# A two-layer hybrid trunk on one core: the modulation stream, the first norm and the front in one block, and the tail of y in the next pair's levels

## The chip, the cores and the metric

The kernel runs on one core of a Trainium2 chip. The metric is the device time of one execution in microseconds (us). Engines: TensorE (PE), VectorE (DVE), ScalarE (ACT), GpSimd (POOL), and SyncE (SP), which issues the DMAs. Each engine takes its instructions in program order; they wait for one another through semaphores.

## The reference

Two layers over a context of 128 tokens and a sample of 512 tokens (T = 640 columns here), width 1024. All in float32.

```python
m = silu(cvec) @ w_mod + b_mod                     # 6 parts of 1024 for each layer
sh1, sc1, gt1, sh2, sc2, gt2 = split(m, 6)
h = rmsnorm(x, norm_mix) * (1 + sc1) + sh1         # the sample also has grid_posemb added to x
# layer 0
proj = h @ w_in;  r, k, v, u = split(proj)         # u: 256 channels, the Fourier mixer's
dh = centred_shift(h) - h
xw, xa, xg = (h + dh * mu_wag[s] for s in range(3))   # go into three low-rank products
ys, s_fin = wkv7_scan(...)                         # 12 heads of 64, forward and backward
y = ys[0] + flip(ys[1])
y = (y - mean(y)) * rsqrt(var(y) + GN_EPS) * gn_w + gn_b      # over each head's 64 channels
bonus = sum(r * k * r_k) * v
out_a = (y + bonus) * (sigmoid(xg @ g1) @ g2)
out_b = real(fft2(u))                              # over tokens and the 64 channels of a group
x = x + gt1 * (concat(out_a, out_b) @ w_out)
# then a mixture of 16 experts; layer 1 has another mixer; a last norm
```

## The kernel before

Channels lie on the 128 partitions: `x` and `h` are [128, 8 chunks, 640]. The program is a row of blocks, and a block starts when every engine has ended the one before.

**setup().** SyncE loads `vec` (160 KB), `cst` (136), the tables (817) and the masks `m32` (768 KB), then 24 slabs of `mod_w` of 2048 KB, each half of one part's 1024 rows, into a ring of six; `x` (2560 KB) after the twelfth. TensorE takes each slab in 8 products with the two conditioning columns (L266) into PSUM rows; ScalarE copies a finished part (L242), TensorE turns it into columns in 8 products (L253, `turn`), VectorE adds the bias (L298). GpSimd adds the position table to `x` (L324, L326). After the last turn, ScalarE squares `x` chunk by chunk (L124) and TensorE sums the squares over the channels in 40 products of one column (L132).

**norm(0, 0).** VectorE and ScalarE make a rate for each token, TensorE spreads the rates over the partitions (L346), VectorE scales `x` into `h`, ScalarE applies gain and shift.

**even_front().** SyncE loads `w1` (1536 KB), `wu` (1024), `dfs` (2048), `dfp` (128) and saves `x`. TensorE computes the 256 channels of `u` (L462, the channel products), transforms them along the width (L470), multiplies the three mixes by `w1` (L482, the low-rank products) and transforms along the tokens (L490, L492). VectorE makes `dh` and the three mixes for all 8 chunks at a time (L435 to L448). ScalarE copies.

**even_heads().** Six pairs of heads, the first five in a loop with `following`, the last apart. For each pair: matrices of all five tiles of 128 tokens (L707), which VectorE masks (L1150, 20 masks); six **levels** of a block-wise inversion, 30 steps of products of 64 (L744, L748), each put in place by a predicated copy of VectorE (L1156), with one chunk of the next pair's key projection (`project(K, 0, ...)`, L639) after every third step; corners (L782); then a **chain** over four steps of tiles: old state (L806, L809) into `rs`, products for `us` (L817), new state (L827, L828), with pieces of the next pair's work (`FILL`, `ahead`) between them; then `y` into PSUM banks 6 and 7 (`pair(3)`). `pair(q)` is banks 2q and 2q + 1. The tail of y before:

```python
dve: yc = y - mean (L1206); [queries() of the next pair]; reciprocal(root) (L1212)
     yc*root (L1214); yc*gn_w+gn_b (L1216); yc+bon (L1218); mix = yc*pair(0) (L1221)
     sem_inc("tail_done"); bonus() of the next pair (L1128, L1129)
pe:  gate -> pair(0); mean -> pair(2); bonus -> pair(1); variance -> pair(3) (L848 to L853)
```

In the next pair TensorE waits for `tail_done` before its third product of `heads`, since its matrices go to banks 4 to 7, and for `bonus_read` before it writes to `pair(1)`.

Of the kernel before, what the change touches and what calls it, by code (L numbers as in the profile page):

```python
# [69 lines left out]
def build(nc, t):  # L70
    ctx = ExitStack()
    with ctx:
# [44 lines left out]
        chunk_sums = ps[:, 7, 384:384 + KC * NT]  # L117
# [10 lines left out]
        def sum_x(pe, sq, m):  # L128

            pe.wait_ge(sem("xsq_ready"), 1).then_inc(sem("xsq_ready"), -1)  # L130
            for tt in range(NT):
                last = pe.matmul(chunk_sums[:, m * NT + tt:m * NT + tt + 1], sq[:, m % 2, tt * P:(tt + 1) * P], mean1024[:, 0:1], start=True, stop=True)  # L132
            last.then_inc(sem("xsq_used"), 1)
# [69 lines left out]
        def setup():  # L203
            cv = Carve()
            ring = cv(6, 4, 1024)
            th = cv(KC, 2)
            scond = cv(KC, 2)
            rows = cv(3, D)
            m32 = cv(LEVELS * 4 * HD)
            sq = cv(2, T)  # L210
            modw = t["mod_w"]

            with stage() as block:
                @block.sync
                def _(sp):
                    sp.dma_start(vec[:, :], t["vec"]).then_inc(sem("vec_in"), 16)
                    sp.dma_start(cst[:, :], t["cst"][:, 0:NKEEP]).then_inc(sem("const_in"), 16)
                    sp.dma_start(work["tables"][:, :], t["cst"][:, NKEEP:]).then_inc(sem("const_in"), 16)
                    sp.dma_start(m32, t["m8"]).then_inc(sem("const_in"), 16)
                    sp.sem_inc(sem("slab_free"), 6)  # L220
                    for l in range(2):
                        for i in range(2):
                            for s in range(3):
                                for k in range(2):
                                    sp.wait_ge(sem("slab_free"), 1).then_inc(sem("slab_free"), -1)
                                    src = modw[l, k * 512:(k + 1) * 512, :].rearrange("(c p) (i s n) -> i s p c n", p=P, i=2, s=3)
                                    sp.dma_start(ring[:, 2 * s + k], src[i, s]).then_inc(sem(f"slab{2 * s + k}"), 16)
                        if l == 0:
# [4 lines left out]
                def _(act):  # L233
# [9 lines left out]
                    for m in range(KC):  # L243
                        square_x(act, sq, m)
# [1941 lines left out]
```

## Time and profile before

| what | us |
|---|---|
| three runs | 2872.93, 2877.30, 2892.89; median 2877.3 |
| the profiled execution, its own time | 2877.23 |
| its span | 2874.5 |
| setup with its column sums, to the first norm | 0 to 164 |
| norm and front | 164 to 259 |
| six pairs of heads | 259 to 1184 |
| output projection, experts, second layer, last norm | 1184 to 2874 |
| from pair to pair: loads of the gate's weights at 454.00 and, four pairs on, 1034.45 | 145.1 each |
| TensorE, VectorE, ScalarE, GpSimd busy | 2437.3, 1796.3, 1250.9, 158.4 |

### The profile page before, as it was taken

The page shows a single profiled execution, that of the slowest core. Times are in us where ns is not written, and L with a number is a line of the kernel's source. Part 1 is how long each engine was busy: PE and PEld are TensorE (multiplying, and loading weights), DVE is VectorE, ACT ScalarE, POOL GpSimd, SP SyncE. Part 2 cuts the span into 40 slices and gives each one's busy share as a digit, 9 for nine tenths or more (in the row PEclk, how much of TensorE's full clock was granted, in tenths as well). Part 3 has the DMA queues.
Part 4 walks back from the last instruction along what each step waited for, and adds up shares of the span by engine and source line. Part 5 has one row for each costly group of instructions (what it writes and reads, how often), then busy time and mean ns, then how long its engine had stood idle before and what let it go on. Part 6 is the DMA issues. An engine that isn't in the chain of part 4 may idle for free. (4 is left out here: it accounts for less than half of the span.)

```text
span 2874.5 us, 51159 instructions
## 1 busy us (share of the span) xinstructions
PE 2437.3 (85%) x19268; PEld 1642.4 (57%) x19268; DVE 1796.3 (62%) x2258; ACT 1250.9 (44%) x1535; POOL 158.4 (6%) x159
## 2 busy tenths in 40 slices
PE   5668787878787876785999999959988599999995
PEld 1244465656565656453666666645545366666664
DVE  0041646464646462127999999937832799999992
ACT  0120232313131311025888888820122587888881
POOL 0100000000000000001000000000000100000000
PEclk8869898889898887787999999959998799999996
DMA  9921101010101000236999999931102699999992
GB/s 392 372 104 26 26 3 28 3 27 3 27 3 27 3 2 3 96 114 253 374 389 386 388 388 386 345 128 39 59 1 111 248 377 387 386 386 388 386 354 82
DMA packets 172542, 539.20 MB, mean 188 GB/s; under 512 B 12449, under 2 KB 43809, under 8 KB 172258
## 3 DMA queue, kind: packets, MB, share of 16 engines
q1 hardware_dynamic: 165858, 514.62, 46.9%
q0 software_dynamic: 6528, 22.29, 3.3%
q8 instruction: 123, 2.02, 0.3%
q14 instruction: 33, 0.27, 0.0%
HBM read 510.28 MB, written 26.61 MB: 187 GB/s over the span
## 5 line engine op out<-in xcount | busy, mean ns | idle before, releaser
L1652 DVE TENSOR_TENSOR wl<-raw,wh 128x1024 fp32r<-128x1024 f32 x768 | 896.1, 1219 | 68.6 <-DVEq L1651 59.8
L1598 ACT ACTIVATE wh<-raw 128x1024 fp32r<-128x1024 f32 x768 | 796.3, 1058 | 198.7 <-ACTq L1597 192.3
L1535 PE MATMUL ps<-wh,xs 128*80 128x512 f32 x3072 | 846.4, 394 | 6.7 <-PEq L1530 6.7
L1535 PEld LDWEIGHTS ps<-wh,xs 128*80 128x80 f32 x3072 | 450.3, 148 | 246.3 <-issue 8.5
L1535 PE MATMUL ps<-wl,xs 128*80 128x512 f32 x1536 | 477.1, 392 | 0.0
L1535 PEld LDWEIGHTS ps<-wl,xs 128*80 128x80 f32 x1536 | 227.8, 148 | 127.7 <-issue 1.2
L1156 DVE COPY_PREDICATED wk<-m,ps 128x512 f32<-128x512 uint8 x180 | 130.9, 731 | 142.0 <-DVEq L1155 141.6
L639 PE MATMUL ps<-h,wk 128*128 128x512 f32 (+1 forms) x576 | 182.7, 460 | 10.0 <-PEq L669 10.0
L940 ACT ACTIVATE wk<-ps 128x256 f32<-128x256 f32 (+1 forms) x180 | 65.8, 365 | 213.7 <-ACTq L939 213.7
L1760 PE MATMUL ps<-h,wk 128*128 128x128 f32 (+1 forms) x512 | 142.4, 440 | 11.1 <-PEq L1790 9.8
L639 PEld LDWEIGHTS ps<-h,wk 128*128 128x128 f32 x576 | 97.3, 199 | 86.3 <-issue 83.5
L707 PE MATMUL ps<-wk 64*128 64x256 f32 x480 | 83.0, 484 | 55.9 <-PEq L701 27.5
L1760 PEld LDWEIGHTS ps<-h,wk 128*128 128x128 f32 x512 | 78.7, 193 | 74.9 <-issue 74.9
L761 PE MATMUL ps<-wk 64*64 64x64 f32 x2400 | 104.6, 221 | 14.8 <-issue 14.7
L266 PE MATMUL ps<-wk 128*2 128x512 f32 x384 | 63.4, 798 | 55.8 <-PEq L263 55.8
L744 PE MATMUL ps<-wk 64*64 64x64 f32 x2400 | 106.4, 225 | 5.1 <-issue 3.7
L748 PE MATMUL ps<-wk 64*64 64x64 f32 x2400 | 103.2, 221 | 2.8 <-issue 2.8
L761 PEld LDWEIGHTS ps<-wk 64*64 64x64 f32 x2400 | 89.8, 137 | 17.6 <-issue 17.3
L707 PEld LDWEIGHTS ps<-wk 64*128 64x128 f32 x480 | 56.9, 235 | 74.4 <-issue 70.2
L1994 DVE SCALAR_TENSOR_TENSOR wk<-wk 128x670 f32<-128x670 f32 x116 | 96.4, 907 | 0.4 <-DVEq L1988 0.4
L1512 POOL DMA_INDIRECT ysum<-rows,idx x32 | 50.8, 1586 | 783.9 <-POOLq L1510 783.9
L744 PEld LDWEIGHTS ps<-wk 64*64 64x64 f32 x2400 | 85.5, 133 | 10.8 <-issue 6.4
(269 smaller groups left out, 2834.9 us busy)
## 6 DMA issues: line engine op xcount, KB each, us to landing
raw<-in_moe_w_gate SPq DMA_DIRECT2D x64, 2048.0 KB, 10.3
raw<-in_moe_w_up SPq DMA_DIRECT2D x64, 2048.0 KB, 11.7
raw<-in_moe_w_down SPq DMA_DIRECT2D x64, 2048.0 KB, 11.3
wk<-in_mod_w SPq DMA_DIRECT2D x24, 2048.0 KB, 23.9
wk<-in_ev_w_in SPq DMA_DIRECT2D x18, 512.0 KB, 6.1
wk<-in_od_w_in SPq DMA_DIRECT2D x4, 2048.0 KB, 16.0
ysum<-raw SPq DMA_DIRECT2D x10, 512.0 KB, 16.8
hrow<-rows SPq DMA_DIRECT2D x10, 512.0 KB, 4.4
```

Source lines behind the costliest of these rows:

```text
L639: last = pe.matmul(pair(q)[:, a:b], win[:, c, s], h[:, c, a:b], start=c == 0, stop=c == KC - 1)
L707: last = pe.matmul(ps[:, 4 + (n + hh) % 4, k * 256:(k + 1) * 256], src[lo:hi, z, tt], ar[lo:hi, z, tt], start=True, stop=True)
L744: pe.matmul(ps[to:te, zb, slotT(z, hh):slotT(z, hh) + HD], lhs, rhs, start=True, stop=True)
L748: last = pe.matmul(ps[to:te, zb + 1, slotN(z, hh):slotN(z, hh) + HD], lhs, rhs, start=True, stop=True)
L761: last = pe.matmul(ps[to:te, 2 + u % 2, at:at + HD], mat[lo:hi, g, z, hh, 0, lo:hi], inv(g, z, hh, lo, hi), start=True, stop=True)
L940: act.activation(yw[:, g].rearrange("p z h n -> p (z h n)")[:, 0:w], ps[:, 2 + u % 2, 0:w], ACT.Copy).then_inc(sem("yw_copied"), 1)
L1156: dve.copy_predicated(xx[:, g].rearrange("p z k h n -> p z k (h n)"), bcast(lv[:, q // NT], 2, 2), ps[:, zbank(q):zbank(q) + 2, 0:4 * HD]. ...
L1535: last = pe.matmul(ps[0:CAP, b0 + k], lhs[:, xk, c, :], w[:, s, a:b], start=c == 0 and xk == 0 and w is wh, stop=c == KC - 1 and xk == 1)
L1598: act.activation(wh[:, n % SPLIT], raw[:, n // 4 % RAW, n % 4], ACT.Copy).then_inc(sem("high_ready"), 1)
L1652: dve.tensor_tensor(wl[:, n % SPLIT], raw[:, n // 4 % RAW, n % 4], wh[:, n % SPLIT].bitcast(F32), ALU.subtract).then_inc(sem("low_ready"), 1)
L1760: last = pe.matmul(pair(q)[:, a:b], win[:, m // 4, c, m % 4 * P:(m % 4 + 1) * P], h[:, c, a:b], start=c == 0, stop=c == KC - 1)
L1994: dve.scalar_tensor_tensor(to, src, cw[:, c, k:k + 1], to, ALU.mult, ALU.add).then_inc(sem("tap"), 1)
```

## The change

`setup()`, `norm(0, 0)` and `even_front()` become one block, `opening()`. The ring has three slabs; `x` is loaded ahead of the slabs and the other inputs and the save of `x` between them; each part has its own product, copy and turn in PSUM banks 6 and 7; the front's work is written between the slabs. `dh` and the mixes are made by chunk (`mixed(c)`), and the low-rank products follow chunk by chunk into three PSUM pairs. In the diff the first `slab(n)` is SyncE's (after n = 5 it loads `dfs` and `dfp`, after 7 `w1`, after 9 `m32`), the second is TensorE's (8 products into banks 6 and 7), and the last piece is VectorE's.

```diff
+        def opening():
+            RING, PARTS = 3, 12
+            dh = cv(2, T)
+            xm = cv(2, 3, T)
...
+                    def slab(n):
+
+                        sp.wait_ge(sem("slab_free"), 1).then_inc(sem("slab_free"), -1)
...
+                    sp.dma_start(x[:, :, :], t["xT"].rearrange("(c p) n -> p c n", p=P)).then_inc(sem("x_in"), 16)
+                    for n in range(2 * PARTS):
+                        slab(n)
+                        if n == 3:
+                            sp.dma_start(wu, t["ev_w_in"][:, 3 * 768:].rearrange("(c p) n -> p c n", p=P)).then_inc(sem("wu_in"), 16)
...
+                        if n == 11:
+                            sp.wait_ge(sem("x_final"), 1).then_inc(sem("x_final"), -1)
+                            sp.dma_start(t["xsave"].rearrange("(c p) n -> p c n", p=P), x[:, :, :]).then_inc(sem("x_saved"), 16)
...
+                    def slab(n):
+
+                        k = n % 2
+                        if k == 0 and n:
+                            pe.wait_ge(sem("mod_read"), 1).then_inc(sem("mod_read"), -1)
+                        pe.wait_ge(sem(f"slab{n % RING}"), 16).then_inc(sem(f"slab{n % RING}"), -16)
...
+                        last.then_inc(sem("slab_free"), 1)
+                        if k:
+                            pe.drain().then_inc(sem("rows_ready"), 1)
...
+                    slab(0)
+                    slab(1)
+                    for m in range(KC):
+                        sum_x(pe, sq, m, SUMS)
+                    turn()
+                    slab(2)
+                    slab(3)
+                    spread_rates(pe)
+                    turn()
+                    channels(0)
+                    channels(1)
+                    slab(4)
+                    channels(2)
+                    channels(3)
+                    slab(5)
+                    channels(4)
+                    channels(5)
+                    turn()
+                    slab(6)
+                    channels(6)
+                    channels(7)
+                    slab(7)
+                    for tt in range(NT):
+                        along_width(tt)
+                    turn()
+                    slab(8)
+                    along_tokens(0)
+                    slab(9)
+                    along_tokens(1)
+                    turn()
+                    slab(10)
+                    slab(11)
+                    for c in range(KC):
+                        low_rank(c)
+                        if c % 2 == 0:
+                            turn()
+                        slab(12 + c)
+                    turn()
+                    for n in range(20, 2 * PARTS):
+                        slab(n)
+                        if n % 2:
+                            turn()
...
+                    mixed(0)
+                    take_mod(2)
+                    mixed(1)
+                    take_mod(3)
+                    take_mod(4)
+                    for c in range(2, KC, 2):
+                        take_mod(4 + c // 2)
+                        mixed(c)
+                        mixed(c + 1)
+                    take_mod(8)
+                    dve.wait_ge(sem("half_sigmoid"), 1).then_inc(sem("half_sigmoid"), -1)
```

In `even_heads()` the tail of y goes in eight pieces behind every third predicated copy of the next pair's levels (`tail`: four reciprocals of 160 of the 640 columns by `y_rate`, then the rest; `y_shifted` is two instructions); ScalarE copies gate and bonus out of PSUM; the variance goes to `pair(1)` and is computed in the next pair's first matrices; the output of pair i is stored in slot (i + 1) % 6 of `mix` and the output projection reads the slots in that order. The first step's old state goes ahead of the levels.

```diff
+                        pe.wait_ge(sem("ymean_read"), 1).then_inc(sem("ymean_read"), -1)
-                                if n == 2:
-                                    pe.wait_ge(sem("tail_done"), 1).then_inc(sem("tail_done"), -1)
...
+                            if tt == 0:
+                                pe.wait_ge(sem("bonus_read"), 1).then_inc(sem("bonus_read"), -1)
+                                y_variance()
...
+                        old_state(0, 1)
...
+                    def tail(n, i):
+
+                        if n < 4:
+                            y_rate(n)
+                        elif n == 4:
+                            y_scaled()
+                        elif n == 5:
+                            y_shifted()
+                        elif n == 6:
+                            y_gated(bass.ds(i, 1))
+                        else:
+                            bonus()
+                            dve.sem_inc(sem("tail_done"), 1)
...
+                            if q % 3 == 2 and q < 3 * KC:
+                                tail(q // 3, i)
```

**TensorE in the stream.** Before, slabs and turns stand alone; the names are the two rings and `tables`, the selector of the turns:

```order
L266 MATMUL ps<-wk 2x512 [waits slab3]
L266 MATMUL ps<-wk 2x512 x7
L253 MATMUL ps<-tables,wk 128x2 [waits rows_copied]
L253 MATMUL ps<-tables,wk 128x2 x7
L266 MATMUL ps<-wk 2x512 [waits slab4]
L266 MATMUL ps<-wk 2x512 x7
L266 MATMUL ps<-wk 2x512 [waits slab5]
L266 MATMUL ps<-wk 2x512 x7
L253 MATMUL ps<-tables,wk 128x2 [waits rows_copied]
L253 MATMUL ps<-tables,wk 128x2 x7
L253 MATMUL ps<-tables,wk 128x2 [waits mod_read,rows_copied]
L253 MATMUL ps<-tables,wk 128x2 x7
```

Now, after the second turn, the channel products stand between turn and slab:

```order
L383 MATMUL ps<-tables,mix 128x2 [waits rows_copied]
L383 MATMUL ps<-tables,mix 128x2 x7
L392 MATMUL ps<-h,wk 128x512 [waits wu_in,h_sample,h_prompt]
L392 MATMUL ps<-h,wk 128x128
L392 MATMUL ps<-h,wk 128x512
L392 MATMUL ps<-h,wk 128x128
L392 MATMUL ps<-h,wk 128x512 [waits h_sample,h_prompt]
L392 MATMUL ps<-h,wk 128x128
L392 MATMUL ps<-h,wk 128x512
L392 MATMUL ps<-h,wk 128x128
L373 MATMUL ps<-wk 2x512 [waits mod_read,slab1]
L373 MATMUL ps<-wk 2x512 x7
```

The column sums and the spread of the rates stand ahead of this piece, where before they came after the last slab.

**VectorE where a pair ends** (`x` holds y, the gate and the root; `mix` the output). Before, from the centring on:

```order
L1206 SCALAR_TENSOR_TENSOR x<-ps,x 128x640 [waits dve_done,y_sbuf_v,ymean_ready]
L1119 TENSOR_TENSOR wk<-x,wk 128x5x128 [waits dve_done]
L1120 TENSOR_TENSOR wk<-x,wk 128x5x128
L1119 TENSOR_TENSOR wk<-x,wk 128x5x128
L1120 TENSOR_TENSOR wk<-x,wk 128x5x128
L1212 RECIPROCAL x<-x 128x640 [waits dve_done,yroot_ready]
L1214 TENSOR_TENSOR x<-x 128x640 [waits dve_done]
L1216 TENSOR_SCALAR x<-x,wk 128x640 [waits dve_done]
L1218 TENSOR_TENSOR x<-x,wk 128x640 [waits dve_done]
L1221 ISA [waits dve_done,gate_ready]
L1221 TENSOR_TENSOR mix<-x,ps 128x640
L1128 TENSOR_TENSOR wk<-ps,x 128x640 [waits dve_done,bonus_sum]
```

Now the queries stand first, then the centring, then the loop's branch and the next pair's state:

```order
L1268 SCALAR_TENSOR_TENSOR x<-x,wk 128x640 [waits dve_done]
L1276 TENSOR_TENSOR wk<-x,wk 128x5x128 [waits dve_done,y_sbuf_v]
L1277 TENSOR_TENSOR wk<-x,wk 128x5x128
L1276 TENSOR_TENSOR wk<-x,wk 128x5x128
L1277 TENSOR_TENSOR wk<-x,wk 128x5x128
L1285 SCALAR_TENSOR_TENSOR x<-ps,x 128x640 [waits dve_done,ymean_ready]
L1434 REGISTER_ALU [waits dve_done]
L1434 COMPARE_AND_BRANCH
L1340 TENSOR_SCALAR wk<-wk 64x64 [waits state_in]
L1341 TENSOR_SCALAR wk<-wk 64x64
L1340 TENSOR_SCALAR wk<-wk 64x64
L1341 TENSOR_SCALAR wk<-wk 64x64
```

The reciprocal and the four steps behind it left this place for the levels.

**TensorE at the start of the chain.** Before, the last three cells of the old state, both low-rank products, then `us` (L817); the row ahead of these waits for the corner copies and the blocks:

```order
L806 MATMUL ps<-wk 128x128
L809 MATMUL ps<-wk 128x64 x2
L806 MATMUL ps<-wk 128x128
L809 MATMUL ps<-wk 128x64 x2
L806 MATMUL ps<-wk 128x128
L809 MATMUL ps<-wk 128x64 x2
L648 MATMUL ps<-lora,wk 128x512
L648 MATMUL ps<-lora,wk 128x128
L648 MATMUL ps<-lora,wk 128x512
L648 MATMUL ps<-lora,wk 128x128
L817 MATMUL ps<-wk 128x64 [waits r_copied]
L817 MATMUL ps<-wk 128x64 x7
```

Now, from the last corners on:

```order
L900 MATMUL ps<-wk 64x64 [waits yw_copied,corner_copied]
L900 MATMUL ps<-wk 64x64 x3
L744 MATMUL ps<-lora,wk 128x512
L744 MATMUL ps<-lora,wk 128x128
L934 MATMUL ps<-wk 128x64 [waits corner_copied,blocks_copied]
L934 MATMUL ps<-wk 128x64 x7
L744 MATMUL ps<-lora,wk 128x512
L744 MATMUL ps<-lora,wk 128x128
L735 MATMUL ps<-h,wk 128x512 [waits e_read]
L735 MATMUL ps<-h,wk 128x128
L735 MATMUL ps<-h,wk 128x512
L735 MATMUL ps<-h,wk 128x128
```

The old state is no longer there, and the second low-rank product stands behind `us` (L934).

## Rows read from the trace of the kernel before

**Rows 1.** Windows, one for each stage up to the end of the front.

```profile
core 0: us, PE busy (x) PEld busy (x) DVE busy (x) ACT busy (x) POOL busy (x), PEclk, DMA share, GB/s
0.00:142.00 142.00, 83.79 (x550) 29.92 (x551) 4.72 (x13) 13.47 (x14) 11.19 (x19) 0.83 0.98 387
142.00:178.00 36.00, 22.89 (x118) 22.48 (x117) 9.67 (x32) 14.04 (x19) 0.00 (x0) 0.54 0.00 0
178.00:259.00 81.00, 66.25 (x220) 35.73 (x220) 32.06 (x43) 9.19 (x13) 0.00 (x0) 0.91 0.25 93
```

**Rows 2.** DMA issues of the stream: line, count, KB each, us to landing.

```profile
2.78 48.87 SPq L227 DMA_DIRECT2D wk<-in_mod_w  x12
...
wk<-in_mod_w SPq DMA_DIRECT2D x24, 2048.0 KB, 23.9
x<-in_xT SPq DMA_DIRECT2D x1, 2560.0 KB, 26.0
```

**Rows 3.** Timeline, TensorE and ScalarE: parts of the stream.

```profile
14.81 3.60 PE L266 MATMUL ps<-wk 128*2 128x512 f32 x16 [14.81 <-PEq L263]
19.93 1.90 PE L266 MATMUL ps<-wk 128*2 128x512 f32 x16 [1.52 <-PEq L263]
...
32.27 1.02 ACT L242 ACTIVATE wk<-ps 98x1024 f32<-98x1024 f32 x1 [9.22 <-ACTq L241]
...
32.36 1.92 PE L253 MATMUL ps<-tables,wk 98*128 98x2 f32 x16 [0.29 <-PEq L251]
```

**Rows 4.** Groups by line between 142 and 259 us.

```profile
L482 PE MATMUL ps<-wk 128*128 128x512 f32 (+1 forms) x96 | 26.7, 436 | 2.0 <-PEq L476 1.5 <-PEq L479 0.4
L462 PE MATMUL ps<-h,wk 128*128 128x512 f32 (+1 forms) x64 | 19.7, 471 | 19.4 <-PEq L458 19.4
...
L490 PE MATMUL ps<-wk 128*128 128x512 f32 x32 | 14.1, 594 | 0.3 <-PEq L486 0.3
...
L470 PE MATMUL ps<-tables,wk 128*128 128x256 f32 x20 | 5.0, 391 | 1.3 <-PEq L464 1.1
```

**Rows 5.** Windows: the column sums, then a pair's levels, then its chain.

```profile
146.00:164.00 18.00, 17.20 (x80) 17.14 (x80) 0.45 (x5) 4.42 (x6) 0.00 (x0) 0.50 0.00 0
...
774.00:822.00 48.00, 42.14 (x1464) 35.34 (x1463) 24.35 (x43) 12.95 (x37) 1.56 (x3) 1.00 0.02 4
824.00:838.00 14.00, 13.55 (x53) 11.18 (x54) 3.37 (x10) 2.84 (x5) 0.00 (x0) 0.51 0.00 1
```

**Rows 6.** Timeline, VectorE, where one pair ends and the next starts.

```profile
740.57 0.82 DVE L1206 SCALAR_TENSOR_TENSOR x<-ps,x 128x640 f32<-128x640 f32 x1 [2.96 <-DVEq L1205]
...
743.84 0.82 DVE L1120 TENSOR_TENSOR wk<-x,wk 128x640 f32<-128x640 f32 x1
746.45 4.15 DVE L1212 RECIPROCAL x<-x 128x640 f32<-128x640 f32 x1 [1.78 <-DVEq L1211]
...
755.57 0.16 DVE L1129 COPY wk<-wk 128x2 f32<-128x2 f32 x1
...
758.12 2.48 DVE L1150 TENSOR_TENSOR wk<-ps,tables 128x512 f32<-128x512 f32 x4 [0.44 <-DVEq L1149]
```

**Rows 7.** Timeline, levels: a predicated copy, and a projection chunk.

```profile
778.96 1.57 DVE L1156 COPY_PREDICATED wk<-m,ps 128x512 f32<-128x512 uint8 x2 [1.74 <-DVEq L1155]
...
786.44 1.35 PE L639 MATMUL ps<-h,wk 128*128 128x512 f32 x4
```

**Rows 8.** Timeline, TensorE, start of the chain over the tiles.

```profile
824.45 0.77 PE L806 MATMUL ps<-wk 128*128 128x128 f32 x2 [1.55 <-PEq L804]
...
832.18 3.67 PE L817 MATMUL ps<-wk 128*128 128x64 f32 x16
...
838.88 0.39 PE L827 MATMUL ps<-wk 128*128 128x128 f32 x2
```

**Rows 9.** The same of the last pair.

```profile
1115.54 0.76 PE L806 MATMUL ps<-wk 128*128 128x128 f32 x2 [1.55 <-PEq L804]
...
1121.88 2.37 PE L817 MATMUL ps<-wk 128*128 128x64 f32 x10 [0.99 <-PEq L813]
```

More of the change, by code:

```diff
@@ L456, in _ @@
                 @block.tensor
                 def _(pe):
-                    pe.wait_ge(sem("wu_in"), 16).then_inc(sem("wu_in"), -16)
-                    for m in range(2):
-                        for a, b in ((0, NS), (NS, T)):
-                            for c in range(KC):
-                                last = pe.matmul(pair(m)[:, a:b], wu[:, c, m * P:(m + 1) * P], h[:, c, a:b], start=c == 0, stop=c == KC - 1)
-                        last.then_inc(sem("u_ready"), 1)
-                    pe.wait_ge(sem("u_sbuf"), 1).then_inc(sem("u_sbuf"), -1)
@@ new lines, in turn, with channels @@
+                    def turn():
+                        pe.wait_ge(sem("rows_copied"), 1).then_inc(sem("rows_copied"), -1)
+                        for j in range(KC):
+                            last = pe.matmul(ps[:, 6, 2 * j:2 * j + 2], rows[0:98, j * P:(j + 1) * P], C("sel")[0:98], start=True, stop=True)
+                        last.then_inc(sem("mod_done"), 1)
+                    def channels(c):
+                        pe.wait_ge(sem("h_sample"), 1).then_inc(sem("h_sample"), -1)
+                        pe.wait_ge(sem("h_prompt"), 1).then_inc(sem("h_prompt"), -1)
+                        for m in range(2):
+                            for a, b in halves:
+                                last = pe.matmul(pair(1 + m)[:, a:b], wu[:, c, m * P:(m + 1) * P], h[:, c, a:b], start=c == 0, stop=c == KC - 1)
+                        if c == KC - 1:
+                            last.then_inc(sem("u_ready"), 1)
@@ L984, in heads @@
                         done("ysq_ready")
[L985 to L987 removed]
+                        if not following:
+                            y_root()
                     copy_raw(K)
@@ L1123, in queries, with y_centred, y_rate @@
                         dve.sem_inc(sem("invT_free"), 1)
+                    def y_centred():
+                        dve.wait_ge(sem("ymean_ready"), 1).then_inc(sem("ymean_ready"), -1)
+                        dve.scalar_tensor_tensor(yc, pair(2), -1.0 / HD, ysb, ALU.mult, ALU.add).then_inc(dve_done, 1)
+                        done()
+                        dve.sem_inc(sem("yc_ready"), 1)
+                    def y_rate(k):
+                        if k == 0:
+                            dve.wait_ge(sem("yroot_ready"), 1).then_inc(sem("yroot_ready"), -1)
+                        dve.reciprocal(root[:, k * 160:(k + 1) * 160], root[:, k * 160:(k + 1) * 160]).then_inc(dve_done, 1)
+                        done()
@@ L2077, in build @@
         with mixer_memory(0):
-            setup()
-            norm(0, 0)
-            even_front()
+            opening()
             even_heads()
```

529 lines of the change are left out of this document (284 added, 245 removed).

## The prediction

> **What bounds the kernel now.** I read the windows by stage first [rows 1], then the timeline inside each stage that the diff touches. In the first 142 us the DMA engines are busy for 0.98 of the time and TensorE for 84 us only: the stream of 24 slabs of modulation weights is the bound, one slab every 5.12 us (the two slabs in [rows 3] start at 14.81 and 19.93). From 142 to 178 us (column sums, then the first norm) the DMA share is 0.00, and from 178 to 259 (the front) it is 0.25 while TensorE works 66 of 81 us. So 117 us of work on TensorE, VectorE and ScalarE stand behind 142 us in which these engines are mostly free, and nothing but the order of the three blocks holds them apart. Later, at each change from one pair of heads to the next, the reader is to see a hole: VectorE's last query product ends at 744.66, the first mask of the next pair's matrices starts at 758.12, and between them lies the tail of y, with a reciprocal of 4.15 us in it [rows 6]. TensorE waits there, since the next pair's matrices need the PSUM banks that the tail still reads. The experts, the odd mixer and the second half of the program are untouched. The chain of waits on the page ends in the last norm and says nothing of these places.
>
> **Opening: what it costs.** The block has one order per engine, so I add TensorE's work at full clock: 24 slabs at 1.90 = 45.6, 12 turns at 1.92 = 23.0 [rows 3]; column sums 17.2 [rows 5], which ran wholly at half clock; the channel products 19.7, of which the first microseconds ran at half clock, so 17.5; the width products 5.0; the token products 14.1 and half a microsecond of their short ones, 14.6; the low-rank products 26.7 [rows 4]. Sum 149.6. To this come:
> - the first slab lands later, since x (2560 KB) now stands ahead of it and the 768 KB of masks don't: 1792 KB more at 2048 KB in 5.12 us [rows 2] is 4.5 us, so 14.8 becomes 19.3;
> - half clock on slabs 0 to 3 and the first turn: a cold slab took 3.60 against 1.90 [rows 3]; three of these and 1.5 for the turn make 6 us;
> - waits on other engines. The parts share one pair of PSUM banks, so a turn waits for ScalarE's copy of 1.02 us wherever no other product stands between (after part 0 and the last three), the next slab waits for VectorE to read the turn, the spread of the rates and h wait for the norm, and slab 20 waits for a VectorE that first waits for ScalarE's three low-rank activations. Six such waits of 1 to 3.5 us, and some ten handshakes of 0.4, are 17 us;
> - half clock at the end, where only slabs and turns are left: four slabs at 1.7 more, 7 us.
>
> Together 149.6 + 19.3 + 6 + 17 + 7 = 199, and with the spread of the rates and the block's end 202 us, against 259 before: **57 us gained**. What is hidden: the DMA stream needs 24 × 5.12 = 123, x 6.4, the other inputs (6617 KB by their shapes) 16.5 and the save of x 6.4, with the start 155 us; it is hidden under TensorE's 202 as long as TensorE frees slabs evenly, because only three slabs fit in the ring now. VectorE's shifts and mixes were 32 us in the front [rows 1] and go by chunk under the slabs and channel products. If that cover were gone they would cost these 32. Bounds: with the sums at a turn's pace (1.92 for 16 passes, so 9.6 for 80) and no cold end, 187; with every slab (1.7 more) and every turn (1.5 more) at half clock, 59 − 13 already counted, 248.
>
> **Pairs: the hole.** In the changed order [the second place of the order] VectorE does the queries while it would wait for the mean of y (a wait of 2.96 before [rows 6]), then centres y (0.82), then goes on. The queries end 2.6 us earlier than before (the centring, 1.0 with its handshake, and part of that wait no longer stand ahead). Behind them come the centring, 1.0, and what stood between the copy at 755.57 and the mask at 758.12, 2.4. So the first mask comes 13.5 − 3.4 + 2.6 = 12.7 us earlier; I take **12.5**. The mask phase gets the variance product and its root, with a ScalarE table load of each kind as before; the phase is VectorE's (20 masks, 2.48 for four [rows 6]), so I cost it at nothing, and at 1.5 if the root comes late. Five changes of pairs have this hole; the first pair has no y ahead of it, and I count nothing there.
>
> **Pairs: the tail in the levels.** Per pair VectorE gets four reciprocals of 160 columns (a quarter of 4.15 and a fixed part, 1.2 with the handshake), and four pieces of 1.0 to 1.8 us: 9.6 us in all. They stand after every third predicated copy, exactly where TensorE does a projection chunk of 1.35 us before the next correction; before, VectorE sat idle there (1.74 in [rows 7]; the eight gaps of that pair are 1.65 to 2.92). In the levels VectorE is busy 24 of 48 us [rows 5]. That is the cover, and it hides nearly all: I take 2 us per pair, bounds 0 and 9.6. The last pair has no projection in its levels, so there I take 3.
>
> **Pairs: the old state.** Its first step (12 products, four cells) starts at 824.45 [rows 8] in a stretch at a clock of 0.51 [rows 5]; in the last pair the same products take from 1115.54 to 1120.9, where an idle of 0.99 begins [rows 9], so 5.3 us. Now they stand ahead of the levels, in a stretch at full clock, at some half of 5.3: **2.4 us lost** there (the wait of half a microsecond ahead of the levels hides a little), and exposed, since the levels wait behind it. In the chain it is gone, one low-rank product fills the wait for the corner copies, and the other goes behind the products of `us`. These started at 832.18 and can start at 824.5; the state products at 838.88 are then preceded by that low-rank product and two chunks: some 833.5. **5.4 gained**; bounds 3 (the clock falls just the same and the fillers run at half) and 9 (it doesn't fall). In the last pair there are no fillers: products of `us` at 1121.88 instead of 1115.54 [rows 9], 6.4 gained.
>
> Sum for the pairs: a middle one gives 12.5 − 2 − 2.4 + 5.4 = 13.5, four of them 54; the first 0 − 2 − 2.4 + 5.4 = 1; the last 12.5 − 3 − 2.4 + 6.4 = 13.5, less 0.7 for ScalarE's extra copy and the split reciprocal in its own exposed tail, 12.8. Together **68 us**. The output projection only reads the slots in another order: nothing.
>
> All in all 57 + 68 = 125 us off the profiled execution's 2877.2, which is the median too: **2752 us**.
>
> **A rule beside the rows.** In [rows 5] TensorE was busy 17.2 of 18 us and stayed at 0.50, the lower level of 1.2 GHz. The Trainium skill says in TensorE: Matmul & The Clock Gate, Part 1, that "activity releases the throttle". By that rule the column sums, which now follow two slabs at once, would climb to 2.4 GHz and the sum above would be some 8 us less, as in the third rival. The trace speaks against it, since here the clock stayed down through 17 us of work.
>
> **Rivals.**
> - Half clock through much of the opening. For it: 12 turns and all column sums stand between the wide products now, and the sums ran at 0.50 from end to end. Against: single turns between wide products kept 1.92 per turn. It costs 15 to 46 us; with 28, 2780. Chance 0.13.
> - The levels don't hide the tail (each piece sits in the chain copy, correction, copy). Then 9.6 per pair instead of 13 in all: 58 − 13 = 45 lost, 2797. Against: VectorE's 50% in the levels. Chance 0.10.
> - Faster clocks: the sums at full pace (8 us), and the chain's fill keeping the clock (4 × 6 us): 2720. Chance 0.13.
> - Slower than before: the ring works one deep. SyncE's order is fixed: a slab whose buffer TensorE frees late holds back every load behind it, and TensorE's order holds the front's work behind each slab. A slab fetched alone takes 5.1 and the start of a transfer (the first was issued at 2.8 and used at 14.8 [rows 2, 3]; less the constants ahead of it, 1881 KB or 4.7, and its own 5.1, that is 2.2): 7.3, and 1.9 to use it. 24 × 9.2 = 221, the rest of TensorE's work 104, start 19, waits 30: 374, which is 115 slower than before and with the pairs' 68 gives 2924. It decides from an opening of 327 us on. Against: three buffers, and TensorE frees a slab about every 6 us. Chance 0.03.
>
> **How the numbers follow.** My forecast has 0.60 and, from the bounds of its terms, 2735 to 2772. With the rivals on both sides the range for 8 in 10 is 2712 to 2795. Within 1% (2848 to 2906) would need most terms to fail together; 1% is about what a measurement of this kernel can tell from no change. Faster 0.94, same 0.03, slower 0.03.
>
> **What would show it.** The last slab's load issued at about 180 us and the pairs' first load at 202 instead of 259; hardly a stretch of DMA at 0.00 before that; the column sums at 0.50 again; from the last query product to the first mask 3 to 4 us instead of 13.5; pair to pair some 131.5 us instead of 145; reciprocals of 160 columns in the levels, with the levels at 50 us rather than 48. I am wrong if TensorE shows long waits for slabs, if the clock stays at 0.50 between channel products, or if the levels grow by more than 4 us.

## The result, and the profile after

| | before | after |
|---|---|---|
| median of four runs on one chip, us | 2883.6 | 2783.9 |
| lowest and highest | 2872.9, 2892.9 | 2776.7, 2797.4 |
| ratio, 95% interval | | 0.9661 [0.9606, 0.9715] |
| the profiled execution, its span | 2874.5 | 2779.9 |
| opening, to the pairs' first load | 259.3 | 207.8 |
| six pairs, to the output projection's first load | 925.0 | 882.8 |
| the rest | 1690.2 | 1689.3 |

The kernel is faster by 3.4%. The profiled executions differ by 94.6 us: 51.4 in the opening (57 forecast), 42.2 in the pairs (68 forecast), 0.9 behind them. Of the 125 us forecast some three quarters came. The measured median lies inside the range of 2712 to 2795, and the forecast of 2752 is 32 us below it.

Windows of the opening, to be held against [rows 1]:

```profile
core 0: us, PE busy (x) PEld busy (x) DVE busy (x) ACT busy (x) POOL busy (x), PEclk, DMA share, GB/s
0.00:142.00 142.00, 109.95 (x574) 60.98 (x574) 29.39 (x64) 28.33 (x36) 11.49 (x19) 0.89 0.86 326
142.00:178.00 36.00, 33.10 (x202) 16.45 (x202) 17.80 (x31) 2.05 (x2) 0.00 (x0) 1.00 0.83 308
178.00:208.00 30.00, 20.59 (x116) 9.65 (x112) 1.54 (x7) 6.46 (x7) 0.18 (x1) 0.65 0.45 168
```

The DMA share is 0.83 where it was 0.00. Of the compute engines TensorE is now the busiest in all three windows. Its timeline there:

```profile
start us, us, engine line op out<-in xcount [idle before <-releaser]
19.56 3.59 PE L373 MATMUL ps<-wk 128*2 128x512 f32 x16 [19.56 <-PEq L370]
24.67 1.90 PE L373 MATMUL ps<-wk 128*2 128x512 f32 x16 [1.52 <-PEq L370]
27.00 14.27 PE L134 MATMUL ps<-mean,mix 128*128 128x1 f32 x80 [0.43 <-PEq L132]
42.65 3.55 PE L383 MATMUL ps<-tables,mix 98*128 98x2 f32 x16 [1.38 <-PEq L381]
...
58.99 7.23 PE L392 MATMUL ps<-h,wk 128*128 128x512 f32 x16 [3.23 <-PEq L389]
...
81.87 3.37 PE L373 MATMUL ps<-wk 128*2 128x512 f32 x16 [0.78 <-PEq L370]
85.17 4.59 PE L392 MATMUL ps<-h,wk 128*128 128x512 f32 x16
89.69 1.90 PE L373 MATMUL ps<-wk 128*2 128x512 f32 x16
...
184.97 6.43 PE L373 MATMUL ps<-wk 128*2 128x512 f32 x32 [2.53 <-PEq L370]
```

A slab takes 1.90 or some 3.4 to 3.6 us, a block of channel products for two chunks 4.59 or 7.23: the same work at one or the other clock, or partly at each. The last twelve slabs' loads on SyncE's queue, and the first load of the pairs:

```profile
110.73 78.32 SPq L314 DMA_DIRECT2D wk<-in_mod_w  x12
207.81 0.34 SPq L682 DMA_DIRECT2D wk<-in_hpv  x1
```

The last of these loads is issued at about 189 (180 forecast), the pairs' first at 207.8 (202 forecast).

The change of pair on VectorE, to be held against [rows 6]: the queries, the centring (L1285), the next pair's state, the first masks (L1352).

```profile
541.04 0.82 DVE L1277 TENSOR_TENSOR wk<-x,wk 128x640 f32<-128x640 f32 x1
542.30 0.82 DVE L1285 SCALAR_TENSOR_TENSOR x<-ps,x 128x640 f32<-128x640 f32 x1 [0.44 <-DVEq L1284]
544.03 0.60 DVE L1340 TENSOR_SCALAR wk<-wk 64x64 f32<-64x64 f32 x1 [0.90 <-DVEq L1337]
...
545.36 0.16 DVE L1343 TENSOR_TENSOR wk<-wk 128x3 f32<-128x3 f32 x1
546.85 1.29 DVE L1352 TENSOR_TENSOR wk<-ps,tables 128x512 f32<-128x512 f32 x2 [1.33 <-DVEq L1351]
```

From the end of the last query product (541.86) to the first mask it is 5.0 us, where it was 13.5. VectorE is ready at 545.5 and waits: TensorE's first matrices (L819) come late, after an idle of 3.97. The centring that they wait for ended at 543.12.

```profile
539.91 1.25 PE L760 MATMUL ps<-x,cst 128*128 128x512 f32 x4
545.12 3.28 PE L819 MATMUL ps<-wk 64*128 64x256 f32 x16 [3.97 <-PEq L810]
```

What TensorE did in between stands in the records of its loop's branch (L990 here, L872 in the kernel before; shortest, median and longest in ns). The fifth is the one that isn't taken, with 76 ns; the four that lead back last 3.3 to 4.8 us, and before the change 3.3 to 4.0.

```profile
L990 PEldq COMPARE_BRANCH  x5: 76/3943/4767, 402.2 to 954.7; - x5
L872 PEldq COMPARE_BRANCH  x5: 76/3417/3953, 454.0 to 1034.4; - x5
```

The levels, as one window (46 us, where [rows 5] has one of 48): VectorE is busy 29.5 us, and the granted clock is 1.00. The start of the chain, against [rows 8], with its windows:

```profile
566.00:612.00 46.00, 40.86 (x1420) 34.08 (x1419) 29.48 (x40) 11.22 (x29) 1.56 (x3) 1.00 0.02 4
...
616.00:620.00 4.00, 3.82 (x16) 2.47 (x16) 1.28 (x2) 1.68 (x5) 0.00 (x0) 0.50 0.02 4
620.00:624.00 4.00, 4.00 (x16) 3.36 (x16) 2.02 (x6) 2.15 (x4) 0.00 (x0) 0.50 0.00 0
```

```profile
616.80 2.50 PE L744 MATMUL ps<-lora,wk 64*128 64x512 f32 x4
619.23 3.67 PE L934 MATMUL ps<-wk 128*128 128x64 f32 x16
622.83 2.50 PE L744 MATMUL ps<-lora,wk 64*128 64x512 f32 x4
625.26 3.57 PE L735 MATMUL ps<-h,wk 128*128 128x512 f32 x8
```

The order is the new one, the clock the old one: the products for `us` take 3.67 in both kernels.

To compare pairs I cut each at five starts on VectorE: the first product of the bonus input (L1268; before L1111), the first mask, the first predicated copy, the first copy of blocks behind the levels (L1367), and the first read of a new state (L1376). The five stretches below are then *change of pair*, *matrices* (with the first old state, where it stands ahead of the levels), *levels*, *chain start* and *chain*. Middle pairs are the second to fifth; the table has their mean, the start of the pairs, and the length of the last pair.

```
                     pairs  change  matri-        chain         pair    last
                      from  of pair ces    levels start  chain  to pair pair
before               259.3    21.4   17.1   44.5   21.9   40.2   145.1  157.4
after                207.8    11.8   21.4   44.1   19.0   41.9   138.1  141.1
opening alone        211.2    21.6   17.2   48.2   21.3   42.1   150.4  157.6
pairs alone          262.2    11.3   20.5   44.3   18.8   42.5   137.3  141.6
old state back       210.2    11.7   17.7   47.8   22.2   40.2   139.6  141.6
loop written out     208.8     9.6   19.5   44.8   19.1   41.9   134.9  141.2
tail before levels   208.1    11.4   26.6   44.7   19.0   41.0   142.6  144.3
wide sums            206.2    11.2   20.4   44.0   19.0   42.0   136.5  138.4
ring of two          217.6    11.7   20.7   44.1   19.3   41.6   137.4  141.9
corner products      212.7    12.4   21.3   43.9   21.4   41.3   140.4  143.4
light fills          209.5    10.9   21.2   44.2   16.3   39.2   131.8  143.5
written out, sums    206.1     9.6   19.2   44.8   19.3   41.2   134.0  140.8
all three            210.4    10.0   19.3   44.3   15.6   39.2   128.4  140.8
```

### The profile page after: what moved, and what is told of

Same layout as the page of the kernel before. It is cut to its first block and busy times, and to the rows that moved or that the text cites. A ratio compares the mean times of both kernels' runs of the same rounds, so it can differ in the third digit from the quotient of the medians.

```text
span 2779.9 us, 51370 instructions
## 1 busy us (share of the span) xinstructions
PE 2430.9 (87%) x19272; PEld 1637.1 (59%) x19272; DVE 1804.9 (65%) x2298; ACT 1262.2 (45%) x1550; POOL 157.5 (6%) x161
## 5 line engine op out<-in xcount | busy, mean ns | idle before, releaser
L735 PE MATMUL ps<-h,wk 128*128 128x512 f32 (+1 forms) x576 | 188.5, 471 | 11.2 <-PEq L765 11.2
L1352 DVE TENSOR_TENSOR wk<-ps,tables 128x512 f32<-128x512 f32 x120 | 74.9, 684 | 32.1 <-DVEq L1351 32.1
L879 PEld LDWEIGHTS ps<-wk 64*64 64x64 f32 x2400 | 86.1, 135 | 16.1 <-issue 16.1
L862 PEld LDWEIGHTS ps<-wk 64*64 64x64 f32 x2400 | 86.5, 134 | 12.7 <-issue 7.7
L819 PE MATMUL ps<-wk 64*128 64x256 f32 x480 | 71.5, 433 | 24.4 <-PEq L810 22.9
L866 PEld LDWEIGHTS ps<-wk 64*64 64x64 f32 x2400 | 86.2, 136 | 7.7 <-issue 7.5
```

The source lines that it names most:

```text
L735: last = pe.matmul(pair(q)[:, a:b], win[:, c, s], h[:, c, a:b], start=c == 0, stop=c == KC - 1)
L819: last = pe.matmul(ps[:, 4 + (n + hh) % 4, k * 256:(k + 1) * 256], src[lo:hi, z, tt], ar[lo:hi, z, tt], start=True, stop=True)
L862: pe.matmul(ps[to:te, zb, slotT(z, hh):slotT(z, hh) + HD], lhs, rhs, start=True, stop=True)
L866: last = pe.matmul(ps[to:te, zb + 1, slotN(z, hh):slotN(z, hh) + HD], lhs, rhs, start=True, stop=True)
L879: last = pe.matmul(ps[to:te, 2 + u % 2, at:at + HD], mat[lo:hi, g, z, hh, 0, lo:hi], inv(g, z, hh, lo, hi), start=True, stop=True)
L1352: dve.tensor_tensor(mat[:, tt, z, hh].rearrange("p k n -> p (k n)"), ps[:, 4 + n % 4], tri[:, z], ALU.mult).then_inc(sem("mat_read"), 1)
```

## The experiments

Each starts from the changed kernel unless it says otherwise. Executions of this program vary: the changed kernel's four runs span 21 us, so a difference between single runs is read from the table above, stretch by stretch, and never from the total alone. Where no ratio is given, there was one run.

**Opening alone, pairs alone.** The block of the opening with the old pairs, and the old first three blocks with the new pairs.

> The new opening with the pairs of before. If the two parts are independent, the pairs' first load comes at 208 us and the pairs take 925 us as before, so some 51 us less than before: a ratio of 0.982. Rival: the opening leaves something behind for the pairs (a table in ScalarE, a clock, a late load); then the pairs take more than 928 us.

> The changed pairs behind the setup, norm and front of before. If the parts are independent, the pairs start at 259 us and take some 883 us instead of 925: 42 us less, a ratio of 0.985. Rival: part of the 42 comes from the opening; then the pairs take more than 890 us.

Three rounds each on one chip: 2844.9 us, ratio 0.986 [0.983, 0.989], and 2835.0 us, ratio 0.9821 [0.9786, 0.9856]. The product of the ratios is 0.968, against 0.966 for both together: within the intervals the two halves of the change add up. The changed pairs took 881.7 us behind the old opening and 882.8 behind the new one, so in them nothing of the gain comes from the opening (883 expected, more than 890 for the rival). The opening alone starts its pairs at 211.2, 48 us earlier than before. In its pairs, whose code is that of before, the profiled execution took 950.9 us and not 925.0: levels of 48.2 instead of 44.5, and a chain of 42.1 instead of 40.2. That is more than the 928 that I had set as the rival's sign. The four runs' median is 40 us below before and not 48, a difference of the size of the interval. Whether the new opening leaves something behind for the old pairs, or the 26 us are the chance of one execution, isn't settled; the next experiment shows where such time goes.

**Old state back in the chain.** The first step's old state is issued where it was, and both low-rank products follow it.

```diff
-                        old_state(0, 1)
...
-                            if j:
-                                old_state(j, 6)
+                            old_state(j, 6)
```

> The changed kernel with the first old state and both low-rank products back in their places at the start of the chain. My theory after the traces: ahead of the levels the move costs 3.3 us in a middle pair (idle of VectorE before the first predicated copy 4.65 instead of 1.31) and gives 2.9 in the chain, so nearly nothing; here a middle pair lasts 138 us plus or minus 1, and only the last pair loses some 3 us. Rival, the prediction's sum: the move is worth 3 us per middle pair, so here 141.

2790.9 us, pair to pair 139.6, between my 138 and the rival's 141; the last pair lost 0.5 and not 3. The matrices are 3.7 us shorter and the chain's start 3.2 longer, as forecast in kind; what I had not on my list is in the levels, 47.8 instead of 44.1. Windows at the start of the second pair's levels, first of this kernel, then of the changed one:

```profile
429.00:435.00 6.00, 3.16 (x113) 2.90 (x108) 2.06 (x3) 0.00 (x0) 0.00 (x0) 0.76 0.02 5
435.00:441.00 6.00, 6.00 (x149) 4.67 (x149) 2.88 (x5) 1.15 (x3) 0.00 (x0) 0.67 0.01 3
```

```profile
429.00:435.00 6.00, 5.07 (x160) 4.05 (x160) 3.09 (x4) 0.98 (x2) 0.00 (x0) 1.00 0.01 3
435.00:441.00 6.00, 5.59 (x202) 4.70 (x200) 3.97 (x5) 1.53 (x4) 0.00 (x0) 1.00 0.02 5
```

Without the old state there, TensorE starts the levels on a clock of 0.67 to 0.76. The opening alone, which also lacks it, does so too; the kernel before, which lacks it as well, doesn't. The first 12 us of a pair's levels, first before (the second pair), then of the opening alone (the third):

```profile
484.60:496.60 12.00, 10.48 (x366) 8.79 (x357) 6.31 (x9) 2.44 (x7) 0.00 (x0) 1.00 0.02 4
```

```profile
591.50:603.50 12.00, 9.20 (x223) 7.18 (x215) 4.39 (x6) 1.54 (x4) 0.00 (x0) 0.72 0.02 4
```

So half clock there makes the levels 3 to 4 us longer (48.2 and 47.8 against 44.5), but that it is the old state's products which keep the clock is not shown: of three kernels without them one kept it. From pair to pair this run is 1.5 us longer than the changed kernel, with 3.7 less in the matrices and 1.7 less in the chain, 3.7 more in the levels and 3.2 more in the chain's start.

**TensorE's loop written out.** The first five pairs are the same instructions without a loop on this engine.

```diff
-                    with pe.Fori(0, HP - 1) as i:
+                    for i in range(HP - 1):
                         heads(True)
```

> The changed kernel with TensorE's loop over the first five pairs written out, so that TensorE has no branch there. Theory: from one pair to the next TensorE loses 3.9 us at its loop's branch (last product ends at 541.2, next starts at 545.1, while what it waits for was ready at 543.3), some 1.8 of it beyond the wait; without the branch the first mask comes 1.5 to 2 us earlier, 9.6 us behind the bonus input as in the last pair instead of 11.8, and a middle pair lasts 136. Rival: the time goes into the half clock after the idle, or instructions are fetched as late without a branch; then nothing changes.

All five changes of pair take 9.6 us, as in the last pair of the changed kernel, to which no branch leads back; the matrices are 1.9 shorter as well. Pair to pair 134.9 instead of 138.1 (136 expected). TensorE at a change of pair:

```profile
544.35 1.25 PE L760 MATMUL ps<-x,cst 128*128 128x512 f32 x4
547.95 2.00 PE L819 MATMUL ps<-wk 64*128 64x256 f32 x16 [2.36 <-PEq L810]
```

The centring that it waits for began at 546.74 and took 0.82, so the first matrix starts 0.4 us behind it, and does so in all five changes. In the changed kernel it starts 2.0 us behind at the change shown above, and 2.0 to 3.5 in the four changes with a branch. The same 16 products also took 3.28 us there, behind the longer idle time, and take 2.00 here. That the branch costs TensorE this time is shown. The total, 2780.5 us, is only 1 us below the changed kernel's profiled execution: the first pair took 6 us longer, with a slow chain (42.7 instead of 39.2), and what stands behind the pairs 3.

**Tail before the levels.** All eight pieces stand between the last mask and the first predicated copy.

> All eight tail pieces stand between the last mask and the first predicated copy instead of behind every third copy. If the levels hide the tail in the changed kernel (my reading, since its levels took no longer than before), this exposes about 9.6 us in each of the five pairs that have a tail: mask to first copy about 30 instead of 21, the levels 42 to 44 as they are without the tail, pair to pair 146 to 148 instead of 138, 40 to 48 us in all. Rival: the pieces sit in the chain of copy and correction and already cost most of their 9.6 us there; then the levels get as much shorter as the stretch before them gets longer, 35 instead of 44 us, and the time stays within 5 us of the changed kernel's 2782.

2812.6 us. The matrices' stretch is 5.2 longer in the middle pairs, and the levels are not shorter (44.7 against 44.1). By themselves these two numbers leave a doubt, since in this kernel the levels start at a lower clock, here in the second pair:

```profile
450.40:462.40 12.00, 11.18 (x297) 9.17 (x301) 4.99 (x8) 1.92 (x5) 0.00 (x0) 0.71 0.02 4
```

But the table has kernels with and without the tail at either clock. At 1.00 the levels take 44.1 with it (changed) and 44.5 without it (before); at the lower clock 47.8 with it (old state back) and 48.2 without it (opening alone). So the levels did hide the whole tail; why this run's took no more than 44.7 at the lower clock isn't shown. The tail costs 5 ahead of them and not my 9.6; the rest fits the 4.65 us that VectorE idled in the changed kernel ahead of the first predicated copy, while TensorE did the old state and the first corrections.

**Wide column sums.**

```diff
-                        sum_x(pe, sq, m, SUMS)
+                        for a, b in halves:
+                            last = pe.matmul(pair(0)[:, a:b], mean1024[:, :], sq[:, m % 2, a:b], start=m == 0, stop=m == KC - 1)
```

> The column sums of the squares are made by 16 products with an all-ones matrix of 128 by 128 over 512 and 128 columns instead of 40 products of one column; they come out spread over the partitions, so the spread of the rates goes too, and the root and two reciprocals of 320 columns take the place of the small ones. If the sums' 14.3 us are their number of passes (80 at 0.18 us), they become some 5 us and the opening gets 9 to 11 us shorter, pairs start at 197 to 199 instead of 207.8. Rival: the opening stood on a wait for h and on half clock there anyway, and the wider work of ScalarE and VectorE gives the gain back: pairs start at 205 or later.

2775.4 us, and my rival's case. The sums took 9.4 us, not 5 (I had counted passes of 0.16; the 32 took 0.29 on average, at full clock), and another wait grew, since VectorE reads the first part only behind the first long reciprocal (2.15 us, up to 44.3):

```profile
29.14 9.38 PE L432 MATMUL ps<-mix,mean 128*128 128x512 f32 x32 [0.43 <-PEq L430]
39.91 1.92 PE L383 MATMUL ps<-tables,mix 98*128 98x2 f32 x16 [1.38 <-PEq L381]
45.16 5.57 PE L373 MATMUL ps<-wk 128*2 128x512 f32 x32 [3.34 <-PEq L370]
```

Pairs start at 206.2, 1.6 earlier than in the changed kernel. Two later kernels with this same opening started them at 206.1 and 210.4, so 1.6 us is inside what chance does here: no gain is shown. The 4.3 us between those two are products on the half clock, one slab in the faster one and, at other places, three blocks of slabs and a turn in the slower. One of these places in the two executions:

```profile
97.58 1.90 PE L373 MATMUL ps<-wk 128*2 128x512 f32 x16 [0.77 <-PEq L370]
```

```profile
97.13 3.28 PE L373 MATMUL ps<-wk 128*2 128x512 f32 x16 [0.77 <-PEq L370]
```

**A ring of two slabs.** `RING` is 2.

> The ring of slabs has two buffers instead of three. If the opening is bound by TensorE's work and the stream has slack (155 of 207 us), a slab waits only where two are freed close together (the last four pairs of slabs, the first ones): 5 to 15 us later, pairs start at 213 to 223. Rival, the slow side of the prediction: the ring's depth is what the opening stands on, a slab goes round in about 9.2 us with one on the way; then the opening grows by 40 us or more, pairs start beyond 248.

Pairs start at 217.6, 9.8 us later: the depth of the ring matters, but a third buffer is worth 10 us and not 40. The total is 2796.9. Ahead of slabs TensorE is idle 37.4 us in all instead of 30.6, the start of some 20 in both, and the slabs themselves take 57.8 instead of 55.1. The slow rival, a ring that works one deep, is refuted even for two buffers.

**Products between the corners, then light fills.** The first adds two products of 512 columns after each corner. The second has one after each of the first four corners, and one ahead of each of two waits in the chain; the results go to free banks and are not used.

```diff
                             corner(g)
+                            if g < 4:
+                                pe.matmul(ps[:, 6, 0:512], headones, h[:, 0, 0:512], start=True, stop=True)
...
+                            if following and j == 1:
+                                pe.matmul(ps[:, 5, 0:512], headones, h[:, 0, 0:512], start=True, stop=True)
                             pe.wait_ge(sem("u_copied"), 1).then_inc(sem("u_copied"), -1)
```

> Two extra products of 512 columns stand after each of the five corners between levels and chain; their result is not used. They take 5 x 0.43 x 2 = 4.3 us at full clock per pair. If the chain's first 10 us run at half clock because of the short corner products and waits ahead of them, the chain's start is at full clock now (low-rank 1.75 instead of 2.50, products for us about 2.0 instead of 3.7) and the pair gets about as much shorter as the extra work costs, within 2 us of the 138.1 from pair to pair. Rival: the clock falls all the same, pair to pair 142 to 144.

> The extra products with unused results are fewer and lie in TensorE's idle time: one of 512 columns (0.95 us) after each of the first four corners, one ahead of the wait for the second step's u, one ahead of the wait for the squares of k. If half clock after idle time is what the chain's start and the stretch at the squares cost, the fills give it back for little: chain start at full clock (5 us for 2.7 us of extra work that isn't hidden), the advance always 39.2 us and not 42.8 in two of three pairs; pair to pair 133 to 135 instead of 138.1, the time 2750 to 2765. Rival: the fills cost what they bring (3.8 us at the corners, 1.9 in the chain), pair to pair 137 to 140, the time within 8 us of 2782.

The first had its work mis-priced: 0.43 us is one pass, and a product is two, so 9.5 us were added per pair (2806.9 us; pair to pair 140.4, between my case and the rival's). The chain's start grew by only 2.4, so 7 us came back, from the idle time at the corners and from the clock, which is 0.93 to 1.00 in the start of the middle pairs' chains where it was 0.57 to 0.71. The second, three rounds: 2764.7 us, ratio 0.9571 [0.9555, 0.9588]; pair to pair 131.8 (133 to 135 expected). Its chain is 39.2 us in every middle pair, and its start is on the full clock (0.90 in one), here in the third pair:

```profile
607.82 1.12 PE L922 MATMUL ps<-h,cst 128*128 128x512 f32 x2
...
613.55 1.34 PE L744 MATMUL ps<-lora,wk 64*128 64x512 f32 x4
614.83 2.00 PE L937 MATMUL ps<-wk 128*128 128x64 f32 x16
616.75 1.34 PE L744 MATMUL ps<-lora,wk 64*128 64x512 f32 x4
```

In the last pair, which has no low-rank products or chunks behind its corners, the chain's start took 16.5 us against 14.1; in the next two kernels, with and without the fills, it took 14.4 and 14.3. What the fills cost there is so between nothing and 2.4.

**All three.** The loop written out with wide sums, and the same with the light fills.

> TensorE's loop over the first five pairs written out, and the column sums by an all-ones matrix; no extra products. If the two gains seen alone (pair phase shorter by about 2 us per change of pair, opening by 1.7 us) add up: 2765 to 2777. Rival: what the loop gave was chance in the half-clock stretches, then 2777 to 2785.

> All three together: fills, TensorE's loop written out, wide sums. If their gains are of different places and add up: 2735 to 2755, the change of pair at 9.6 us and the advance at 39.2 us in every pair, and a smaller spread between runs than the changed kernel's 21 us. Rival: the fills only move half clock to another place (start of the levels, end of the opening), then 2760 to 2775.

On the chip of the light fills: 2771.5 us, ratio 0.9596 [0.9579, 0.9614], and (five rounds) 2746.7 us, 2742.1 to 2750.8, ratio 0.9508 [0.9491, 0.9524]. The last is the fastest kernel here, 1.6% below the changed kernel by the ratios, with intervals that don't touch. Between the two the fills are the only difference: 24.8 us. The interval of the first overlaps the changed kernel's, so a gain of the loop and the sums is shown for the change of pair alone, not for the total. The change of pair is 9.6 us in all ten cases but one, 11.1, where VectorE waits 1.5 us longer ahead of the queries; TensorE's first matrix is 0.4 behind the centring there too.

## Why the prediction came out as it did

The sign, the two halves and the range held, and the opening's sum was sound. The pairs gave 42 of 68 us: the hole and the chain's start were priced too high, the old state's cost too low, and the chain behind its start, which I had at nothing, grew. One term erred the other way, the tail in the levels. The range held by its width, since the pairs' sum was 1.6 times what they gave.

- **Opening, 51 instead of 57.** TensorE's work was right: up to 208 us it is busy 163.6 us, against 149.6 + 6 + 7 and 1.4 of the spread, 164.0. The parts shifted among themselves: channel products 21.0 and not 17.5, column sums 14.3 and not 17.2. The start was 19.6 (19.3). What is left, 24.6 us of idle time behind the start and the block's end, I had at some 19: the waits were the mis-sized term, with 3.2 for `h` and 2.5 ahead of slab 20 as the longest.
- **The hole, 10.0 instead of 12.5** (mean of five changes of pair). The last pair's was 11.5, the middle ones' 9.7. I added up VectorE's work and took TensorE to be there. In the middle pairs it wasn't: its way back through the loop's branch, 3.3 to 4.0 us before too, had lain under VectorE's tail, and became the wait that ends last. The loop written out shows its price: 2.2 us per change of pair; the matrices were 1.9 shorter too, and 3.2 are left from pair to pair.
- **The tail in the levels.** I charged 2, in the last pair 3; it cost nothing. The levels were 0.3 shorter, in the last pair 1.7, and the comparison at either clock shows that the cover is whole.
- **Old state ahead of the levels, a loss of 4.2 instead of 2.4** in the middle pairs, 2.8 in the last. With the loop written out it is 2.4, the price that I had for the twelve products. With the branch, but the old state back in the chain, the stretch is only 0.6 longer than before. The two together so cost 1.2 more than each alone; why isn't shown.
- **Chain start, 2.9 instead of 5.4.** This is the lower bound, and its reason held: "the clock falls just the same and the fillers run at half". The light fills, which keep the clock, make it 5.6, and the last pair, without fillers, had 6.7 for 6.4. So the price holds where the fillers don't run at half clock.
- **The rest of the chain, 1.7 longer; I had 0.** The chain takes 39.2 or some 43, in both kernels. In the slower case the clock is down for some 10 us; here in the changed kernel, where it falls in the second of two short idle times (1.14 and 1.48 us, up to 503.2 and 505.8):

```profile
500.00:504.00 4.00, 2.86 (x20) 2.27 (x20) 0.18 (x2) 2.06 (x4) 1.53 (x3) 1.00 0.00 0
504.00:508.00 4.00, 2.52 (x7) 1.26 (x5) 2.75 (x5) 1.23 (x2) 0.03 (x1) 0.59 0.00 0
508.00:514.00 6.00, 6.00 (x19) 4.22 (x18) 3.17 (x2) 4.45 (x5) 0.00 (x0) 0.50 0.00 0
```

It happened in one of four middle pairs before and in three of four in the changed kernel, in 27 of 44 over all the kernels without fills in the chain, and in none of the eight of the two with them. Products at the corners alone don't prevent it (two of four, in the run between corners), so it is the two products in the chain's waits, 1.9 us of otherwise idle time, that take it away. Why one execution has it and the next, with the same instructions, hasn't, stays open.

A middle pair so gave 7.0 instead of 13.5: 9.7 − 4.2 + 0.3 + 2.9 − 1.7. The last gave 16.3 instead of 12.8: 11.5 − 2.8 + 1.7 + 6.7 − 0.8. The first lost 2.1 and didn't gain 1: 3.7 more in its matrices, and 1.6 ahead of its bonus input, which I had not counted, against 3.3 less in its change, levels and chain start. Four times 7.0, 16.3 and −2.1 are the 42.2.

The rivals: of the half clock through the opening a part is real, chance slabs of some 1.5 us each, but TensorE's work came out as forecast, so not the 15 us from which I counted it. The tail is hidden, so the second falls. The faster clocks didn't come by themselves. The ring is refuted above.

On the column sums I had set the trace against a rule of the Trainium skill (TensorE: Matmul & The Clock Gate, Part 1), that "activity releases the throttle". The changed kernel says more: here the sums begin on the full clock, with slabs ahead of them, and lose it in the middle of unbroken work.

```profile
27.00:30.00 3.00, 3.00 (x27) 3.00 (x27) 0.00 (x0) 1.25 (x2) 0.00 (x0) 1.00 1.03 410
30.00:33.00 3.00, 3.00 (x17) 3.00 (x17) 0.00 (x0) 1.10 (x3) 0.00 (x0) 0.54 1.02 407
33.00:36.00 3.00, 3.00 (x15) 3.00 (x16) 0.00 (x0) 1.33 (x2) 0.00 (x0) 0.50 1.08 358
```

TensorE is busy in 3.00 of 3.00 us in each, and the granted clock goes from 1.00 to 0.50. With the wide sums in the same place it stayed at 1.00 from 29 to 42 us. So this case doesn't bear the rule out, if the profile's busy time is read as its activity: two stretches of busy time at one place had different clocks.

## What to carry to other kernels

When a stretch of one engine is taken off the path, ask what the other engines did behind it before you count all of it as gained: TensorE's branch lay in the 4.37 us of idle time ahead of the first matrices in the trace of before (at 748.35), and cost nothing until the tail had gone. Where TensorE comes out of many short products and waits, price what follows at the half clock even if it is dense, and try a wide product without use in the idle time ahead of it: six of them per middle pair, some 6 us of work, brought 5.6 us net with the loop written out. Compare such kernels stretch by stretch, as here the totals of one kernel's runs differ by 21 us.

## What I had not expected of the hardware

- The branch back in TensorE's loop over the pairs, some 1900 recorded passes a round, lasts 3.3 to 4.8 us, and the first product came 2.0 to 3.5 us behind the work that it waited for; without the branch it comes 0.4 behind. In the same trace the loop at L1747, some 320 passes a round, takes 0.2 us to go back.
- The granted clock fell from 1.00 to 0.50 under 9 us of unbroken one-column products.
- The same instructions at the same place run at either clock from execution to execution: a slab after an idle of 0.77 took 1.90 in one and 3.28 in another.
- The same code of the pairs took 925 us in one profiled execution and, behind the new opening, 951 in another.
